# First attention: the softmax reciprocals move from the weights to the gate, and GpSimd's work in the stage is exchanged

## The reference, cut to what matters

```python
s_win = jnp.einsum('bqkgd,bjkd->bkgqj', qb, kb) * scale     # masked outside +-WINDOW
s_ctx = jnp.einsum('bqkgd,bjkd->bkgqj', qb, k_ctx) * scale
p = sink_softmax(jnp.concatenate([s_ctx, s_win], axis=-1), sink_b)
return jnp.einsum('bkgqj,bjkd->bqkgd', p, vals)
...
o = window_attention(q, k, v, k_ctx, v_ctx, sink_logit[i])
y = (o * jax.nn.silu(g)) @ w_out_c[i]
```

## Time and profile before

| | us |
|---|---|
| median of three runs | 2332.96 |
| span of the profiled execution, 32528 instructions | 2329.2 |
| PE busy in it | 2224.6 (96%) |
| DVE busy | 1585.5 (68%) |
| POOL busy | 1529.4 (66%) |
| ACT busy | 855.4 (37%) |

### The profile page before, as it was taken

How to read it: one execution, slowest core, us unless ns; L and a number is a source line. 1 busy time by engine, 2 the same in 40 slices (tenths; PEclk the granted TensorE clock), 3 DMA queues, 4 the chain that set the end, 5 groups by cost and what they waited for, 6 DMA issues and landing times.

```text
span 2329.2 us, 32528 instructions
## 1 busy us (share of the span) xinstructions
PE 2224.6 (96%) x11183; PEld 1856.4 (80%) x11183; DVE 1585.5 (68%) x2296; ACT 855.4 (37%) x1538; POOL 1529.4 (66%) x1401
## 2 busy tenths in 40 slices
PE   5999999999999999999999988899999999999998
PEld 3788889888888877777877867777788888888887
DVE  3855665668795699986899969877887344444434
ACT  3331112223221688862343447833421222222223
POOL 2655556745994788746789854357788766666652
PEclk8999999999999999999999989999999999999999
DMA  9445445514467556534343486553442211111152
GB/s 361 116 127 172 131 139 166 183 49 156 140 192 231 166 159 177 136 100 177 87 131 108 143 210 156 142 185 104 165 131 91 67 55 55 55 55 54 55 181 91
DMA packets 197729, 314.33 MB, mean 135 GB/s; under 512 B 34044, under 2 KB 86968, under 8 KB 196288
## 3 DMA queue, kind: packets, MB, share of 16 engines
q1 hardware_dynamic: 161520, 221.43, 33.1%
q10 hardware_dynamic: 36048, 90.82, 10.5%
HBM read 251.34 MB, written 60.85 MB: 134 GB/s over the span
## 4 chain that ended last, share of the span: by engine, by line
PE 51%; DVE 9%; issue 3%; POOL 2%; ACT 2%; DMA 1%; SPq 0%; ACTq 0%; DVEq 0%; POOLq 0%
PE PS L1405 14%; PE PS L1407 14%; PE PS L1406 14%; PE PS L1830 2%; DVE PS L3298 1%; POOL ACC L1340 1%; PE PS L1819 1%; DVE PTL L3353 1%; DVE PB L3373 1%; PE PS L1820 1%; DVE TT L3122 1%; PE PS L1893 1%; PE PS L1881 1%; DVE HXL L2729 0%; PE PS L1883 0%
## 5 line engine op out<-in xcount | busy, mean ns | idle before, releaser
L1405 PE MATMUL PS<-HXH,WH 128*128 128x512 f32 x1664 | 658.5, 396 | 25.9 <-DVE HXL L2866 5.5
L1406 PE MATMUL PS<-HXL,WH 128*128 128x512 f32 x1664 | 651.5, 392 | 0.0
L1407 PE MATMUL PS<-HXH,WL 128*128 128x512 f32 x1664 | 651.0, 391 | 0.0
L1236 POOL TENSOR_TENSOR WL<-RAW,WH 128x512 fp32r<-128x512 f32 x400 | 569.4, 1424 | 33.3
L1233 POOL TENSOR_SCALAR WH<-RAW 128x512 fp32r<-128x512 f32 x400 | 315.6, 789 | 413.5 <-PE PS L1407 247.5
L1405 PEld LDWEIGHTS PS<-HXH,WH 128*128 128x128 f32 x1664 | 314.6, 189 | 99.6 <-DVE HXL L2866 5.5
L1407 PEld LDWEIGHTS PS<-HXH,WL 128*128 128x128 f32 x1664 | 314.5, 189 | 66.4
L1406 PEld LDWEIGHTS PS<-HXL,WH 128*128 128x128 f32 x1664 | 314.8, 189 | 66.0 <-issue 1.9
L3166 DVE TENSOR_TENSOR Y<-PS,Y 128x1024 f32<-128x1024 f32 x56 | 68.5, 1224 | 101.4 <-PE PS L1407 101.4
L1382 POOL TENSOR_SCALAR PB<-PB,RC 128x640 f32<-128x640 f32 (+1 forms) x128 | 99.1, 783 | 49.5 <-DVE RC L3383 49.4
L1405 PE MATMUL PS<-AHH,WH 128*128 128x512 f32 x320 | 124.9, 390 | 0.8 <-ACT Y L2393 0.4
(11 more groups left out here) (413 smaller groups left out, 4815.9 us busy)
## 6 DMA issues: line engine op xcount, KB each, us to landing
RAW<-in_ada_w SPq DMA_DIRECT2D x160, 256.0 KB, 2.8
RAW<-in_w_in_ab SPq DMA_DIRECT2D x88, 256.0 KB, 2.7
XX<-XR ACTq DMA_DIRECT2D x4, 4096.0 KB, 14.4
RAW<-in_w_in SPq DMA_DIRECT2D x56, 256.0 KB, 2.7
RAW<-in_w_ffn_in SPq DMA_DIRECT2D x112, 128.0 KB, 2.2
RAW<-in_w_ffn_out SPq DMA_DIRECT2D x54, 256.0 KB, 3.6
XR<-XX ACTq DMA_DIRECT2D x3, 4096.0 KB, 13.4
RAW<-in_w_in_c SPq DMA_DIRECT2D x40, 256.0 KB, 2.7
```

Source lines behind the costliest of these rows:

```text
L1236: g.tensor_tensor(WL[:, sw, 0:m], raw_of(n)[:, 0:m], WH[:, sw, 0:m].bitcast(F32), ALU.subtract).then_inc(gpsimd_done, 1)
L1405: mm(out, wh, xh, start=first, stop=False, **kw)
L1406: mm(out, wh, xl, start=False, stop=False, **kw)
L1407: return mm(out, wl, xh, start=False, stop=last, **kw)
```

## The change

The reciprocals no longer scale the weights. DVE takes the four reciprocals of a block in one instruction at slot 4z + 5. POOL spreads them to 64 columns a head (RCB, 128x256). PE turns that in two transposes (slots 4z + 10 and 4z + 11) into unused columns of the score banks, and DVE multiplies them into the gate GT (two products of 128x128 a block). The turns wait for the exponential alone.

Of the key tiles of a block, the first (`POOL_C`) is now split by POOL: ACT copies it to PTF, POOL makes high and low part, and its product with the values comes four slots behind the turn instead of three. POOL also does the product OT x GT, at `GATE_AT` = 15, which is slot 4z + 15 of every fourth block (not for the last group, which stays with DVE). The ada tiles have slots of their own (`ADA_AT`), 48 of them from slot 4 to slot 123.

On SyncE `load_g(b)` and `load_q(b)` now stand together, gate first, ahead of the ada tile c for which `ADA_AT[c - 4]` is at least 16b - 14; that is c = 10, 17, 23, 29, 35 and 42 for b = 2 to 7. `load_g(b)` waits for POOL's product of group b - 2.

```diff
+        PTF = [at(f"PTF{b}", [HALF], F32, EX + 4096 + 2048 * b) for b in range(4)]
+        RCB = [at(f"RCB{b}", [4, 64], F32, EX + 12288 + 1024 * b) for b in range(2)]
...
+        POOL_C = (0,)
+        C_LAG = {x: 4 if x[1] in POOL_C else PV_LAG["c"] for x in TILES["c"]}
+        SPREAD_C, PRODUCTS_C = spread("c"), {}
+        for u0, xs_ in sorted(SPREAD_C.items()):
+            for x in xs_:
...
+        ADA_AT = [u0 for u0 in range(4, 124) if u0 % 4 == 0 or (u0 % 4 == 3 and u0 // 4 % 5 < 3)][:48]
+        GATE_AT = 15
+        SCALES = {}
+        for z in range(32):
+            for r in range(2):
+                SCALES[{30: 128, 31: 130}.get(z, 4 * z + 10) + r] = (z, r)
...
-                    sp.wait_ge(vector_done, upto("og", b - 2))
+                    sp.wait_ge(*of("og", b - 2))
...
+            ATT_LOADS = {}
+            for b in range(2, 8):
+                c = next((x for x in range(4, 48) if ADA_AT[x - 4] >= 16 * b - 14), 48)
+                ATT_LOADS.setdefault(c, []).append(b)
...
-                if 0 <= c <= 48 and c % 8 == 0:
-                    if c // 8 < 6:
-                        load_g(c // 8)
-                    else:
-                        load_q(7)
-                        load_g(6)
-                        load_g(7)
-                        load_rows(1)
-                if 0 <= c < 48 and c % 8 == 4:
-                    load_q(c // 8 + 1)
+                if c == 0:
+                    load_g(0)
+                    load_g(1)
+                if c == 4:
+                    load_q(1)
+                for b in range(2, 8):
+                    if c in ATT_LOADS and b in ATT_LOADS[c]:
+                        load_g(b)
+                        load_q(b)
+                if c == 48:
+                    load_rows(1)
...
-                    for s in range(32):
-                        i = s % 8
-                        lo = 129 if i in (0, 7) else 1
-                        for h in range(4):
-
-                            pool.wait_ge(vector_done, upto("rc", "c", 4 * s + h))
-                            x = PB[s % 2][:, h, lo:641]
-                            g.tensor_scalar(x, x, RC[s % 2][:, h:h + 1], 1.0, ALU.mult, ALU.mult).then_inc(gpsimd_done, 1)
-                            did(gpsimd_done, ("P", "c", s, h))
...
+                    def split_tile(z, ti):
...
+                        pool.wait_ge(scalar_done, upto("ptf", z, ti))
+                        if tb >= PT_RING["c"]:
+                            pool.wait_ge(products_done, upto("pvt", "c", tb - PT_RING["c"]))
+                        g.tensor_scalar(PTH[:, w_, :], PTF[z % 4][:, :], 1.0, 0.0, ALU.mult, ALU.add).then_inc(gpsimd_done, 1)
+                        did(gpsimd_done, ("pth", "c", tb))
+                        pool.wait_ge(gpsimd_done, upto("pth", "c", tb))
+                        g.tensor_tensor(PTL[:, w_, :], PTF[z % 4][:, :], PTH[:, w_, :].bitcast(F32), ALU.subtract).then_inc(gpsimd_done, 1)
+                        did(gpsimd_done, ("ptl", "c", tb), ("ptf_free", z))
+
+                    def spread_reciprocals(z):
+
+                        pool.wait_ge(vector_done, upto("rc", "c", z))
+                        if z >= 2:
+                            pool.wait_ge(products_done, upto("rb", z - 2, 1))
...
+                                        ALU.mult, ALU.mult).then_inc(gpsimd_done, 1)
+                        did(gpsimd_done, ("rcb", z))
+
+                    for u in range(4 * 31 + 9):
+                        z = step_at(u, 5, 32)
+                        if z is not None:
+                            spread_reciprocals(z)
+                        for z, ti in SPREAD_C.get(u - 1, []):
+                            if ti in POOL_C:
+                                split_tile(z, ti)
+                        z = step_at(u, GATE_AT, 32)
+                        if z is not None and z % 4 == 3:
+                            b = z // 4
+                            pool.wait_ge(vector_done, upto("ota", z))
+                            pool.wait_ge(vector_done, upto("gr", z, 1))
+                            g.tensor_tensor(OT[b % 2][:, :, :], OT[b % 2][:, :, :], GT[b % 2][:, :, :], ALU.mult).then_inc(gpsimd_done, 1)
+                            did(gpsimd_done, ("og", b))
+                        if u in ADA_AT:
+                            if u >= 8:
+                                pool.wait_ge(vector_done, upto("mx", "c", u - 4))
+                            ada_tile(*left[ADA_AT.index(u)])
...
+                        if z >= 30:
+                            pe.wait_ge(vector_done, upto("gr", z - 1, r))
+                        pe.wait_ge(gpsimd_done, upto("rcb", z))
+                        nc.tensor.transpose(PS[:, 2 * r + 1, 384:HALF],
+                                            RCB[z % 2][:, 2 * r:2 * r + 2, :].rearrange("p h d -> p (h d)"),
+                                            IDF[:, :]).then_inc(products_done, 1)
+                        did(products_done, ("rb", z, r))
...
+                            if u in SCALES:
+                                turn_reciprocals(*SCALES[u])
+                            if u - 2 in SCALES:
+                                pe.wait_ge(vector_done, upto("gr", *SCALES[u - 2]))
...
 
...
+                            pe.wait_ge(*of("ptl", "c", tb))
...
-                                pe.wait_ge(vector_done, upto("ptl", "c", tb - 2))
...
-                                pe.wait_ge(gpsimd_done, upto("P", "c", z, hh))
+                                pe.wait_ge(scalar_done, upto("exp", "c", 4 * z + hh))
...
+                            else:
+                                pe.wait_ge(vector_done, upto("gr", 31, 1))
...
+                if ti in POOL_C:
+                    if z >= 4:
+                        act.wait_ge(gpsimd_done, upto("ptf_free", z - 4))
+                    A(PTF[z % 4][:, :], PS[:, 4 + tb % 2, :], ACT.Copy).then_inc(scalar_done, 1)
+                    did(scalar_done, ("ptf", z, ti), ("turned", "c", tb))
+                    return
...
-                act.wait_ge(vector_done, upto("og", b))
+                act.wait_ge(*of("og", b))
...
-                if i == 3 and b < 7:
-                    gated(b)
...
                         w_ = tb % PT_RING["c"]
+                        if ti in POOL_C:
+                            return
...
-                        if 1 <= u <= 128:
-
-                            y, b, hh = u - 1, (u - 1) // 4 % 2, (u - 1) % 4
-                            dve.wait_ge(scalar_done, upto("exp", "c", y))
-                            if y >= 8:
-                                dve.wait_ge(gpsimd_done, upto("P", "c", y // 4 - 2, hh))
-                            v.reciprocal(RC[b][:, hh:hh + 1], SU[b][:, hh:hh + 1]).then_inc(vector_done, 1)
-                            did(vector_done, ("rc", "c", y))
+                        z = step_at(u, 5, 32)
+                        if z is not None:
+                            dve.wait_ge(scalar_done, upto("exp", "c", 4 * z + 3))
+                            if z >= 2:
+                                dve.wait_ge(gpsimd_done, upto("rcb", z - 2))
+                            v.reciprocal(RC[z % 2][:, :], SU[z % 2][:, :]).then_inc(vector_done, 1)
...
+                        if u in SCALES:
+                            z, r = SCALES[u]
+                            b = z // 4
+                            dve.wait_ge(products_done, upto("rb", z, r))
+                            dve.wait_ge(g_loaded[b % 2], upto("gl", b))
+                            x = GT[b % 2][:, r, z % 4 * P:(z % 4 + 1) * P]
+                            v.tensor_tensor(x, PS[:, 2 * r + 1, 384:HALF], x, ALU.mult).then_inc(vector_done, 1)
+                            did(vector_done, ("gr", z, r))
```

More of the change, by code:

```diff
@@ L752, in program @@
         TB = {w: {x: n for n, x in enumerate(TILES[w])} for w in "cf"}
+        POOL_C = (0,)
[3 more added lines that the diff above has]
+            for x in xs_:
+                PRODUCTS_C.setdefault(u0 + C_LAG[x], []).append(x)
+        FIRST_C, LAST_C = {}, {}
+        for u0 in sorted(PRODUCTS_C):
+            for x in PRODUCTS_C[u0]:
+                FIRST_C.setdefault(x[0], x)
+                LAST_C[x[0]] = x
+        ADA_AT = [u0 for u0 in range(4, 124) if u0 % 4 == 0 or (u0 % 4 == 3 and u0 // 4 % 5 < 3)][:48]
[4 more added lines that the diff above has]
+                SCALES[{30: 128, 31: 130}.get(z, 4 * z + 10) + r] = (z, r)
         def tile_count(z, which):
@@ L1374, in _ @@
                 if e["kind"] == "attc":
[L1375 to L1385 removed]
+                    def split_tile(z, ti):
+                        tb = TB["c"][z, ti]
+                        w_ = tb % PT_RING["c"]
+                        pool.wait_ge(scalar_done, upto("ptf", z, ti))
[6 more added lines that the diff above has]
+                        did(gpsimd_done, ("ptl", "c", tb), ("ptf_free", z))
@@ L1809, in _ @@
                             did(products_done, ("sc", "c", u))
```

(15 more changed lines are left out.)

6 lines of the change are left out of this document (5 added, 1 removed).

## The result

The changed kernel takes 2403.48 us (median of four runs, 2401.81 to 2405.40), the kernel before 2333.0 beside it. The ratio is 1.0303, with a 95% interval from 1.0288 to 1.0317: 70.5 us slower. Forecast were 43 us more, 2376, in a range up to 2398. The direction was right and the size was not; the time lies outside the range.

The account below looks back on a forecast made before the run. DVE was taken as the engine others wait for, the rest close behind. QS stands 31 us (after pace gained within them) plus ada tiles 16 minus 4 gained outside made 43 us more: 2376 us, range 2346 to 2398.

Parts of the forecast that it names:

- stands for QS, with their restart: TensorE's scores at slot 16b wait for QS loads queued behind the gate load: 7.6 us, 5.2 lost net, six times.
- ada tile ahead of the split: POOL does late ada tiles before the split TensorE wants: 3.5 us for b = 2, 5, 7, 5.7 for b = 6; 16 us.
- pace of all slots: Attention slots take 1.83 us instead of 1.98, a block 7.3 instead of 7.93 us.
- The load: On SyncE's queue, eight QS loads take 11.5 us from first issue plus 1.3 for GT, complete at 18.6 us.
- The product: POOL's OT x GT takes 2.6 us behind a split of 2.1, ending 5.3 us after the scores of slot 16b - 6 start.
- The ada tile: As a sign in the trace: four times TensorE's product from POOL's tile waits 3 to 6 us.
- The pace: TensorE's own work is 6.85 us a block, 7.13 with two more turns; all four engines come to 6.7 to 7.2.
- POOL is late at the product as well: Rival: POOL ends each group with a backlog, 2 us more a group and longer stands at the split; 2400 us, chance 0.08.
- The pace isn't gained: Rival: slots stay at 1.98 us, QS stands are 6.7 us, 16 slots take 38.4; 2389 us, chance 0.12.
- The bound from above: Upper end of the range: 40.2 us for 16 slots, 51 us lost, with 18 of the second effect; 2402 us.

Follow-up runs that it names:

- q_first: The changed kernel with the QS loads of a group placed ahead of its gate load in SyncE's queue; 2345.4 us, ratio 1.0055.
- q_first_ada_behind: The changed kernel with QS loads ahead of the gate load, and late ada tiles of groups 2, 5, 6 and 7 moved behind POOL's split; 2324.21 us, ratio 0.9975.
- store_late: The changed kernel with ACT's store of OT ten slots later, for groups 0 to 5; 2397.82 us, ratio 1.0279.
- warm_long: The changed kernel with 88 unread matmuls ahead of TensorE's wait for QS in six slots; 2401.05 us, ratio 1.0304.
- apart: The changed kernel with QS loads placed for slot 16b - 16 and the gate load for slot 16b - 4; 2323.62 us, ratio 0.9960.
- no_turns: The changed kernel with QS and gate loads placed apart, without TensorE's two turns of the spread reciprocals a block; 2320.09 us, ratio 0.9947.
- apart_gate_dve: The changed kernel with QS and gate loads placed apart, and the product OT x GT back on VectorE; 2332.63 us, ratio 1.0002.
- warm: The changed kernel with 64 unread matmuls ahead of TensorE's wait for QS in six slots; 2408.79 us, ratio 1.0326.
- queue_gate_dve: The changed kernel with its queue order kept and the product OT x GT alone back on VectorE; 2370.66 us, ratio 1.0155.

## Why the prediction was right in kind and wrong in size

The mechanism was right: the gate load's new wait on a product that GpSimd makes late, the QS loads queued behind it, and POOL's ada tile behind those. What failed are sizes of the sum. The load was put at 13.2 us from GT's issue and took 15.2; TensorE's own work was put at 6.85 us a block and is 7.46, so that the pace gained 6 to 9 us and not 19; and the half clock behind each stand had no term at all and costs 8 to 11 us. Three experiments share the measured time out over the forecast's three terms:

| | forecast | measured | from |
|---|---|---|---|
| stands for QS, with their restart | 6 x 7.6 = 46 | 58 | changed kernel less q_first |
| ada tile ahead of the split | 16 | 21 (19 by the ratios) | q_first less q_first_ada_behind |
| pace of all slots | -19 | -9 (-6 by the ratios) | q_first_ada_behind less before |
| sum | 43 | 70.5 | |

The kernel before that ran beside q_first_ada_behind had a median of 2330.9 us instead of 2333.0, hence the second figures. The first and the last term are off by 12 and by 10 us or more, which is beyond the noise; the second is not.

**The load.** "QS is complete at 5.8 + 11.5 + 1.3 = 18.6", or 13.2 us from GT's issue. The six groups took 14.5 to 16.1, 15.2 in the mean (group 5 took 16.0). The step left out that ACT's store waits for the same product, and so starts in the same instant; store_late prices that at 1.6 of the missing 2.0 us. The waits for QS are 53.4 us instead of 46, 1.3 a group and not 2.0, since TensorE arrives later than the 11.0 us that were counted (11.8 in group 5). The rule of the Trainium skill that HBM binds at 358 GB/s (DMA: Bandwidth & Descriptors, Bandwidth) helped in neither direction: QS moved at 234 to 242 GB/s here too, far below it. In 954 to 955 us, with GT coming in and OT going out, 410 GB/s stand in the row, above it and below the 435 that the same page gives for the fabric. The page gives the 358 for two cores of a domain that stream at once, and here one core ran.

**The half clock.** The sum has no term for it. The stands are 53.4 of the 58 us, but q_first also waits 15.0 us for POOL's split where the changed kernel waits 8.9. So 58 - 53.4 + 6.1 = 11 us are left for the restart at half clock, an estimate from these rows; the stretches of warm_long gave 8.

**The product.** Estimated at 2.6 us between 2.3 and 2.8, measured 2.40; its end was put 5.3 us behind the start of the scores of slot 16b - 6. In group 5 these start at 944.52 and it ends at 950.66, 6.1 us. The split took 1.9 us of the 2.0 that were counted, the spreading 0.40 of 0.45, the gate product on DVE 0.29 of 0.29:

```profile
L1412 POOL TENSOR_TENSOR PTL<-PTF,PTH 128x512 fp32r<-128x512 f32 x32 | 41.1, 1283 | 2.7
...
L1409 POOL TENSOR_SCALAR PTH<-PTF 128x512 fp32r<-128x512 f32 x32 | 20.3, 633 | 4.7 <-ACT PTF L2012 2.4 <-PE PS L1842 2.3
L3472 DVE TENSOR_TENSOR GT<-PS,GT 128x128 f32<-128x128 f32 x64 | 18.3, 286 | 0.2 <-PE PS L1842 0.2
...
L1420 POOL TENSOR_SCALAR RCB<-RC 128x256 f32<-128x256 f32 x32 | 12.9, 404 | 41.3 <-PE PS L1873 21.2 <-PE PS L1842 9.4 <-DVE RC L3464 9.2
```

So no price of an instruction failed; the ones that failed are of transfers and of slots.

**The ada tile.** Forecast were four waits for POOL's split of 3 to 6 us. The changed kernel shows only 8.9 us in five, since its slots run at half clock behind the stand and hide a part; with the clock held (warm_long) it is 13.3, without stands (q_first) 15.0, of the 19 to 21 us that moving the tiles gives back. The half clock, not counted in the forecast, and this wait cover one another, which is why neither can be read off the changed kernel's own trace.

**The pace.** This is the step that failed in its reasoning and not only in a size: "TensorE idles 28.6 + 4.4 + 1.6 = 34.6 us over 32 blocks, so its own work is 6.85 us a block". Those are rows of PEld, the weight loads, which wait while a matmul still runs. The matmul's own row for the same releaser is half as long, and a window of the kernel before, 820 to 1010 us, puts TensorE at 178.8 of 190:

```profile
PE PS L1830 <- DVE PTL L3353: 13.2, 29, 1.2
```

```profile
820.00:1010.00 190.00, 178.78 (x1117) 151.71 (x1116) 178.34 (x457) 160.05 (x354) 147.37 (x167) 1.00 0.54 147
```

That is 7.46 us busy of 7.93 a block. A pace of 7.3 with two turns more was never to be had; apart runs at 30.5 / 4 = 7.6 with TensorE busy 97.5%, and without the turns (no_turns) a block still takes 7.5. DVE came out at 163.0 / 185 x 7.63 = 6.7 us a block, well under the 7.19 counted, and it did not matter. Of the two causes given for the gain, the product off VectorE brings all of it (apart_gate_dve against apart), and the rest of the exchange, scaling out and splits and turns in, comes to nothing that the runs can tell: 2332.6 against 2332.9.

**The rivals.** "POOL is late at the product as well", 2400 us at 0.08, came closest in its number, by another way: the product was 0.8 us late and not 2. "The pace isn't gained", 2389, was half true. The bound from above, 51 + 18 us lost, came to 2402, and the range was drawn in to 2398; without the store and the restart in it, even the bound ends 1.5 us short of the result.

## What to carry to other kernels

In an in-order DMA queue a wait belongs to everything behind it. Before a load is put next to another for tidiness, compare the time from the end of what it waits for to the landing of the last load behind it with the time until that is needed; and look who else is released by the same event, since those transfers then share the engines. Read an engine's spare time from its busy time over a window, and not from the waits of its weight loads.

## What the runs showed of the hardware

- The granted clock was 1.00 until 960 us with TensorE idle from 956.4, then 0.91 and 0.50 from 961 to 974, over eight microseconds of which it worked again. Over the six groups it was back 3 to 12 us behind the restart. In warm it fell to 0.50 at 967 though TensorE had worked until 964.7. In q_first, waits of TensorE of 1.8 to 4.0 us have some 3 us at 0.50 beside them.
- GpSimd's product of two 128x1024 tiles takes 2.40 us, VectorE's 1.33, 1.8 times as long. The Trainium skill's figure for operations with two inputs is about twice (GPSIMD Engine Reference, Engine selection); the rows agree roughly.
- Eight QS loads are issued in 5.1 us before, and in 5.9 behind the freed gate load in the changed kernel (951.11 to 957.05 us). In store_late it is 6.1 (950.47 to 956.55), so the store is not what slows the queue. Nor is the gate load ahead of them: in queue_gate_dve it is 5.2 (862.67 to 867.87). What it is stays open.
